# State-space loop of a two-layer trunk: one gated unit's low half split in four and moved, and five weight loads moved in SyncE's queue

## What is computed

```python
h = rmsnorm(x, mix_norm_o[j])
y = s5_grouped(h, s5_lam_re[j], ..., s5_d[j])     # y = Re(C h) + D u, h by a scan over the frames
g = jax.nn.gelu(y).astype(x.dtype) @ w_glu[j]     # 2048 x 4096
val, gate = jnp.split(g, 2, axis=-1)
x = x + val * jax.nn.sigmoid(gate)
```

## Time and profile before

| what | value |
|---|---|
| runs of the kernel before | 1984.15, 1987.4, 1989.51 us, median 1987.4 |
| profiled execution, span from first to last instruction | 1982.2 us |
| profiled execution's own time | not listed apart; the three runs lie 2.0, 5.2 and 7.3 us above the span |
| PE busy | 1953.0 us, 99% of the span |
| DVE busy | 1251.1 us, 63% |
| ACT busy | 916.4 us, 46% |
| POOL busy | 648.3 us, 33% |
| mean granted PE clock | 0.995 |

### The profile page before, as it was taken

One profiled execution on the slowest core, in us unless ns is written; L12 is line 12 of the kernel. 1 busy time (PEld: TensorE's weight loads), 2 busy tenths in 40 slices (PEclk: granted clock), 3 DMA queues, 4 the chain that ended last, 5 costly groups with the idle time before them and its releaser, 6 DMA issues.

```text
span 1982.2 us, 31585 instructions
## 1 busy us (share of the span) xinstructions
PE 1953.0 (99%) x11578; PEld 1651.1 (83%) x11578; DVE 1251.1 (63%) x1378; ACT 916.4 (46%) x1222; POOL 648.3 (33%) x858
## 2 busy tenths in 40 slices
PE   8999999999999999999998999999999999999999
PEld 7888788888888888888877888888888888888887
DVE  6885768755765576566559655576556556655654
ACT  6467654443443444344453544544344434434443
POOL 3592439778687778440019300000000000000000
PEclk9999999999999999999998999999999999999999
DMA  7644576666666666686788666655665666566654
GB/s 226 181 134 144 175 197 194 204 231 210 206 210 224 211 204 232 206 268 193 251 281 303 183 183 199 184 181 192 193 192 188 195 195 188 190 196 183 197 194 162
DMA packets 285582, 400.19 MB, mean 202 GB/s; under 512 B 23328, under 2 KB 185264, under 8 KB 283408
## 3 DMA queue, kind: packets, MB, share of 16 engines
q1 hardware_dynamic: 278032, 371.77, 59.7%
q0 software_dynamic: 5216, 24.52, 4.0%
q10 hardware_dynamic: 2208, 2.11, 0.3%
HBM read 371.87 MB, written 25.17 MB: 200 GB/s over the span
## 4 chain that ended last, share of the span: by engine, by line
PE 92%; DVE 2%; ACT 2%; DMA 1%; POOL 1%; issue 1%; SPq 0%; ACTq 0%; DVEq 0%; POOLq 0%
PE ps L729 27%; PE ps L730 13%; PE ps L681 12%; PE ps L683 12%; PE ps L682 12%; PE px L1059 1%; PE px L1061 1%; PE px L1060 1%; PE ps L1059 1%; PE ps L1060 1%; PE ps L1061 1%; PE px L945 1%; DMA raw<-in_w_up_dram 1%; PE ps L666 1%; DVE Wl L1585 1%
## 5 line engine op out<-in xcount | busy, mean ns | idle before, releaser
L1585 DVE TENSOR_TENSOR Wl<-raw,Wh 128x1024 fp32r<-128x1024 f32 x660 | 843.6, 1288 | 616.9 <-ACT Wh L1160 614.6
L1160 ACT ACTIVATE Wh<-raw 128x1024 fp32r<-128x1024 f32 x660 | 691.8, 1059 | 750.7 <-PE ps L683 377.3
L729 PE MATMUL ps<-A,Wh 128*128 128x512 f32 x2364 | 830.1, 396 | 2.7 <-DVE A L1672 2.3
L730 PE MATMUL ps<-A,Wl 128*128 128x256 f32 x2364 | 657.6, 278 | 0.0
L729 PEld LDWEIGHTS ps<-A,Wh 128*128 128x128 f32 x2364 | 443.3, 188 | 108.7 <-issue 5.1
L730 PEld LDWEIGHTS ps<-A,Wl 128*128 128x128 f32 x2364 | 444.7, 188 | 0.3
L681 PE MATMUL ps<-Wh,A 128*128 128x512 f32 x1024 | 399.8, 390 | 0.0
L683 PE MATMUL ps<-Wh,A 128*128 128x512 f32 x1024 | 398.5, 389 | 0.0
L682 PE MATMUL ps<-Wl,A 128*128 128x512 f32 x1024 | 398.4, 389 | 0.0
L683 PEld LDWEIGHTS ps<-Wh,A 128*128 128x128 f32 x1024 | 192.2, 188 | 40.3
L681 PEld LDWEIGHTS ps<-Wh,A 128*128 128x128 f32 x1024 | 192.2, 188 | 39.9
(11 more groups left out here) (376 smaller groups left out, 2035.5 us busy)
## 6 DMA issues: line engine op xcount, KB each, us to landing
raw<-in_w_up_dram SPq DMA_DIRECT2D x256, 512.0 KB, 3.9
raw<-in_w_down_dram SPq DMA_DIRECT2D x256, 512.0 KB, 3.9
raw<-in_w_glu_dram SPq DMA_DIRECT2D x64, 512.0 KB, 4.4
raw<-in_w_in_e_dram SPq DMA_DIRECT2D x52, 512.0 KB, 3.9
raw<-in_w_out_e_dram SPq DMA_DIRECT2D x32, 512.0 KB, 3.8
s_params<-stg POOLq DMA_DIRECT2D x16, 1024.0 KB, 6.1
slot<-s_params SPq DMA_DIRECT2D x12, 768.0 KB, 7.3
slot<-s_params SPq DMA_DIRECT2D x12, 256.0 KB, 7.5
```

What stands on the lines that cost most here:

```text
L729: mm(ps[:, b + t, :], Wh[:, s, c, cols], A[:, k, :], start=(n == 0), stop=False)
L730: last = mm(ps[:, b + t, 0:L], Wl[:, s, c, cols], A[:, k, 0:L], start=False, stop=(n == KC - 1))
L1160: fn(Wh[:, s], raw[:, s], ACT.Copy).then_inc(hi_split, 1)
L1585: tt(Wl[:, s], raw[:, s], Wh[:, s].bitcast(F32), ALU.subtract).then_inc(lo_split, 1)
```

## The change

On DVE, the low half of unit 3 leaves step 1. It is cut in four parts of 128x256 elements, and one part each is issued behind scan(8), scan(9), scan(10) and scan(11). On SP, the load of unit 7 moves from ahead of the loop to step 12, behind the store of y(12). The loads of units 8 and 9 move ahead of the store of y(15), and that of unit 10 ahead of the load of yt(15). The loads of units 11 to 15 stay where they were.

```diff
-            for u in range(2 * NU):
+            for u in range(2 * NU - 1):
                 load_glu(0, u)
             sp.wait_ge(rss_ready, 1)
...
             for c in range(KC):
+                if c == KC - 1:
+                    load_glu(0, 2 * NU)
+                    load_glu(0, 2 * NU + 1)
                 sp.wait_ge(s5_ge, c + 1)
                 sp.dma_start(y_d[c].rearrange("(t q) (j n) -> (q j) t n", t=TPC, j=CT), yb[:, c % 2])\
                     .then_inc(y_stored[c % 2], 16)
...
                     load_rows(c + NSLOT + 2)
+                if c == 12:
+                    load_glu(0, 2 * NU - 1)
                 if c >= 1:
                     load_turned(c - 1)
+            load_glu(0, 2 * NU + 2)
             load_turned(KC - 1)
-            for u in range(2 * NU, 4 * NU):
+            for u in range(2 * NU + 3, 4 * NU):
                 load_glu(0, u)
...
+            def split_quarter(g, s, n):
+
+                dve.wait_ge(hi_split, g * NU + (s + 1))
+                part = tt(Wl[:, s, n], raw[:, s, n], Wh[:, s, n].bitcast(F32), ALU.subtract)
+                if n == UK - 1:
+                    part.then_inc(lo_split, 1)
+
             s5_rotate(0)
             dve.wait_ge(pp_zero, 1)
             for c in range(KC):
-                if c == 1:
-                    split(P_GLU, 3)
                 if c + 1 < KC:
                     s5_rotate(c + 1)
                 s5_scan(c)
+                if 8 <= c < 8 + UK:
+                    split_quarter(P_GLU, 3, c - 8)
             for s in range(NU):
                 split(P_GLU + 1, s)
```

## The result

The changed kernel is slower by a little: 1988.63 us median of 21 runs (1986.16 to 1991.49), against 1985.38 us median of 21 runs of the kernel before (1983.05 to 1989.51). The ratio is 1.0017, with a 95% interval of 1.0011 to 1.0022, so +3.3 us by the medians. The larger set of runs put the kernel before 2 us under the median of the first three. The profiled execution has a span of 1985.0 us, against 1982.2.

A forecast was written before the change was run, and what follows sets the result against it. It took DVE to bound the first half of the state-space loop and PE the second. The terms, -3.6 + 0.2 + 3.3 + 2.3 = +2.2 us, on a median of 1987.4 gave 1989.6 us, range 1982.5 to 1994.5.

The forecast's parts named there:

- Term 1: Loop, step 1: with the split gone, DVE's later work moves forward, kept until PE takes over at step 8; -3.6 us.
- the forecast for in(13): Sign in the changed trace: PE's in(13) at step 13 starts near 1083.0, against 1086.37 before.
- Term 2: Loop, steps 8 to 11: the four quarters and the first one's wait for POOL slightly exceed DVE's lead on PE; +0.2 us.
- rule of one operation: Quarters on DVE: each waits only for the POOL operation that is running; 0.8 us of wait at the first quarter.
- Rival C: First quarter, step 8: DVE waits for all of POOL's step 8 work, as at 1043.15; +2.4 us, 1992.0, chance 0.14.
- D: Steps 8 to 11: POOL holds the port at every quarter; +5.5 us on top of Rival C, 1997.5, chance 0.07.
- Term 3: Tail: loads moved on SP delay the y(15) store, the yt(15) load and ACT reaching unit 8; PE resumes +3.3 us later.
- Term 4: Tail: after standing idle 4.3 us in one piece before unit 8, PE's clock drops; +2.3 us.
- Rival A: Tail: y(15) is not held up or PE's wait stays near 1 us; change -3.6, 1983.8, chance 0.22.
- B: Tail: it is late but PE's clock holds; change -0.1 us, 1987.3, chance 0.13.
- E: Loop: DVE starts 3.6 us early, but PE at half clock takes it back by step 8; 1993, chance 0.04.

The follow-up runs named there:

- e5: e1 with the second parameter load of a step cut from 768 KB to 384 KB from step 6 on, using an earlier step's output weights and direct term; ratio 0.9987.
- e3: The changed kernel with ACT making the high halves of units 8 and 9 ahead of high(14) and high(15); 1981.49 us, ratio 0.9986 to the kernel before.
- e9: e1 with the low half of unit 3 in two parts of 128x512 behind scan(8) and scan(9); ratio 0.9993 to the kernel before.
- e11: e1 run once more, unchanged, beside e12 on one chip; 1982.38 us, ratio 0.9985 to the kernel before.
- e6: e1 with the low half of unit 3 in one piece behind scan(8) instead of four quarters; ratio 0.9990 to the kernel before.
- e7: The kernel before with the low half of unit 3 at step 1 cut in four parts, one behind the other; ratio 0.9999 to the kernel before.
- e12: The kernel of e3 run once more, unchanged, beside e11; 1980.38 us against 1985.18 of the kernel before, ratio 0.9979.
- e1: The changed kernel with the loads of units 8 to 10 put back, keeping the quarters and unit 7's load at step 12; 1982.04 us against 1984.69 before, ratio 0.9987.
- e2: The kernel before with only the loads of units 8, 9 and 10 moved as in the change; 1990.88 us, ratio 1.0035 to the kernel before.
- e8: The changed kernel with only unit 8's load ahead of the store of y(15), units 9 and 10 behind the load of yt(15); ratio 1.0007 to the kernel before.

## Why the prediction was right, and where its sizes were off

The forecast was +2.2 us; the runs give +3.3 and the stage in the trace +3.4. The path was right at each of its steps, and two sizes were off. The forecast time of 1989.6 us is only 1.0 us from the 1988.63 measured by luck: the median it was built on, 1987.4, was 2.0 us above that of the larger set (the runs with both numbers on record lie only 1.7 to 1.9 us above their own spans, not 5.2), which made up for a change that was forecast 1.1 us too small.

- **Term 1** (-3.6): right at DVE, -3.59 by step 8. That it is "kept until PE takes over at step 8" was the weak sentence. PE lost 1.1 us of it on the way, to a gap in its issue and 3.4 us at clock 0.50. I had looked for a late operation and for PE's clock at the start of the loop, which returned at 1049.8 instead of 1057.4 as expected, but not at gaps in PE's own issue. That the forecast for in(13), "near 1083.0", looks met by 1082.53 is chance: 1.40 us of it stood there before the loop. In e5, e3, e9 and e11 the loop's gain at in(13) is 3.2 to 3.5 us, so the term can come out nearly whole.
- **Term 2** (+0.2): right in size. The first quarter took 1.18 us, forecast as 0.8 + 0.35, the others 0.41 to 0.49. In the changed kernel PE was late by more than this, so it cost nothing there; in e5, where PE was not late, in(13) at -3.4 is the forecast of terms 1 and 2. The rule of one operation, on which it rested, is wrong as a rule: e6 waited for four, e7 for two, and the first quarter of e12 for four. Rival C did not come about in the profiled execution, and did in e12: its quarter took 2.6 us longer, the wait that C had worked out, and in(13) came as much later than in e3. (C's price should be those 2.6 us in full, 1992.2 and not 1992.0, as the 0.2 taken off was no part of them.) That the changed kernel's own trace shows one operation is thus partly luck. D did not come about: the later quarters took under 0.6 us.
- **Term 3** (+3.3): the path y(15), yt(15), high(15), table, unit 8 is the chain in the trace. Idle time grew by 4.0 us, 0.7 more than forecast: y(15) took 5.58 us where my working had 4.8, because unit 9's load, right ahead of it, took 5.6 us, not the 4.9 of my working. In e12 that load did take 4.9 us, and y(15) then took 4.8. The load of unit 7 at step 12, costed at nothing, cost nothing: in e1, which has it, PE's only wait for a low half from 1050 to 1120 is the 1.1 us before unit 8.
- **Term 4** (+2.3): PE ran 4.0 us at clock 0.50 and, at about half pace, lost some 2 us. Terms 3 and 4 together are 5.6 forecast and 5.8 measured (-2.5 at unit 7 to +3.4 at unit 12; to the hundredth, -2.47 and +3.36).
- **Rival A**, the free tail, falls with e2, and **B**, a clock that holds, with the row at 0.50. **E** did not happen in the profiled execution, though the trace of e8, whose loop is the changed kernel's, has the clock take the loop's whole gain.

The errors did not cancel: terms 1 and 2 were 0.9 us too good (-3.4 forecast, -2.5 kept by PE), the tail 0.2 us too cheap, and both point the same way.

## What to carry to other kernels

Before a large load is moved ahead of a small store on the same queue, follow the small one to the engine that waits for it and read what that engine does next in its program: here a function table load and the very operation that the large load was to speed up. Do not price a DVE operation beside a busy POOL from one execution: at one place of one program the same quarter took 1.1 to 1.2 us in seven executions and 3.8 in an eighth. Where a change has a gaining and a losing half, run each half alone before judging the whole: here the whole lost 3 us, one half alone gained 3 and the other lost 6 to 7, and the whole with ACT's order mended gained 3 to 4.

## What the runs showed of the hardware that was not expected

- DVE's wait for POOL has no fixed length in POOL operations, and neither the place nor the size of the DVE operation fixes it. A difference of two operands in SBUF waited at step 8 for one POOL operation with 128x256 elements in seven executions (1.13 to 1.18 us long), for four in an eighth (3.82 us), for one with 128x512 (1.41 us) and for four with 128x1024 (4.62 us). At step 1 it waited for two with 128x256 (2.40 us) and for three with 128x1024 (3.66 and 3.65 us in two kernels), while 128x1024 beside other POOL operations waited for one. The Trainium skill (SBUF — State Buffer, "Who interferes with whom") calls the shared port pair an exclusive lock that whoever issues first holds for one whole instruction. The long waits above disagree with it: POOL operations that began after DVE's were served first. What decides stays open.
- PE can stand 1 to 2 us in the middle of a group of products with no semaphore to wait for. Such gaps, of 0.4 to 4.1 us in sum ahead of in(13), are in every trace but that of e5, whose parameter loads are lighter (216 GB/s against 308 in the changed kernel); that the load on the DMA engines is the cause is not shown.
- The first 512 KB load took 4.1 to 5.0 us when it stood ahead of a y transfer (seven kernels) and 3.8 to 4.2 when it stood behind all of them (the other seven). With two loads ahead of it a 128 KB store took 4.8 to 5.8 us, always landing 0.4 to 0.5 us behind the second of them, and 2.2 us with none.
